# The place of the early row sums on VectorE in the last four expert pairs of an RWKV-7, convolution and mixture-of-experts step

## What is computed

```
h = silu(x @ w_gate[e]) * (x @ w_up[e]);  h = h * gate[token, e]
routed = sum over experts of h @ w_down[e]
y = residual + routed + shared;  out = rmsnorm(y)
```

## Time and profile before

| | |
|---|---|
| median of three runs | 1115.92 us (1115.02 to 1118.81) |
| the profiled execution | 1116.3 us |
| its span, first to last instruction | 1114.5 us |
| TensorE busy | 961.8 us, 86% of the span |
| VectorE busy | 536.9 us, 48% |
| GpSimd busy | 349.2 us, 31% |
| ScalarE busy | 226.5 us, 20% |
| mean granted TensorE clock | 0.94 of full speed |

### The profile page before, as it was taken

How to read it: one execution, slowest core, us unless ns; L and a number is a source line. 1 busy time by engine, 2 the same in 40 slices (tenths; PEclk the granted TensorE clock), 3 DMA queues, 4 the chain that set the end, 5 groups by cost and what they waited for, 6 DMA issues and landing times. The chain is left out here.

```text
span 1114.5 us, 17730 instructions
## 1 busy us (share of the span) xinstructions
PE 961.8 (86%) x7221; PEld 560.4 (50%) x7221; DVE 536.9 (48%) x1021; ACT 226.5 (20%) x469; POOL 349.2 (31%) x396
## 2 busy tenths in 40 slices
PE   5999999999999976598998888987988878789896
PEld 4878777877877774257433333333333323333231
DVE  2158759767875867945531101111112334434685
ACT  3241134125113412221111111111111111111012
POOL 0059609914960992001011101011012323312330
PEclk9999999999999999789999988989989888979999
DMA  8645244344524191654699999999999999999931
GB/s 224 187 127 182 96 131 167 110 131 137 181 96 134 61 345 35 246 234 162 262 367 416 418 417 412 412 406 402 403 398 408 400 392 364 403 415 402 390 99 40
DMA packets 98971, 295.65 MB, mean 265 GB/s; under 512 B 19602, under 2 KB 50900, under 8 KB 82231
## 3 DMA queue, kind: packets, MB, share of 16 engines
q1 hardware_dynamic: 80695, 254.02, 60.1%
q0 software_dynamic: 18192, 40.46, 9.7%
HBM read 284.12 MB, written 36.30 MB: 288 GB/s over the span
## 5 line engine op out<-in xcount | busy, mean ns | idle before, releaser
L1278 PE MATMUL bank<-big 64*64 64x64 f32 (+7 forms) x6778 | 905.7, 364 | 129.0 <-DMA big<-in_w_up 72.4
L1278 PEld LDWEIGHTS bank<-big 64*64 64x64 f32 (+3 forms) x6778 | 512.4, 150 | 473.9 <-issue 384.5
L1569 ACT ACTIVATE big<-bank 128x256 f32<-128x256 f32 (+6 forms) x284 | 121.7, 450 | 715.4 <-PE bank L1278 398.9
L1075 POOL DMA_INDIRECT big<-xg,big x32 | 32.4, 1012 | 405.5 <-PE bank L561 354.1
L919 DVE TENSOR_TENSOR big<-big,bank 128x256 f32<-128x256 f32 x32 | 13.5, 420 | 239.5 <-ACT big L1569 239.5
L2039 POOL TENSOR_SCALAR big<-big 128x256 f32<-128x256 f32 x120 | 126.8, 1057 | 1.7
L2051 POOL TENSOR_TENSOR big<-big 128x256 f32<-128x256 f32 x120 | 86.7, 723 | 0.3
L1835 DVE SCALAR_TENSOR_TENSOR big<-big 128x256 f32<-128x256 f32 x120 | 79.2, 660 | 4.1
L979 DVE SCALAR_TENSOR_TENSOR big<-big 128x1024 f32<-128x1024 f32 (+1 forms) x48 | 61.5, 1280 | 16.4 <-DMA big<-yrows,big 13.1
L1092 POOL DMA_INDIRECT big<-yrows,big x48 | 50.3, 1047 | 50.9 <-DVE big L979 28.5
L1569 ACT ACTIVATE big<-big 128x16 f32<-128x16 f32 (+6 forms) x95 | 42.5, 487 | 57.5 <-DVE big L1790 18.5
(11 more groups left out here) (163 smaller groups left out, 412.0 us busy)
## 6 DMA issues: line engine op xcount, KB each, us to landing
big<-in_w_gate SPq DMA_DIRECT2D x64, 1024.0 KB, 15.5
big<-in_w_up SPq DMA_DIRECT2D x64, 1024.0 KB, 20.4
big<-in_w_down SPq DMA_DIRECT2D x64, 1024.0 KB
big<-in_w_in SPq DMA_DIRECT2D x29, 1024.0 KB, 5.5
yrows<-big POOLq DMA_DIRECT2D x32, 512.0 KB, 3.7
big<-in_w_out SPq DMA_DIRECT2D x2, 2048.0 KB, 16.7
big<-in_state_wkv SPq DMA_DIRECT2D x32, 64.0 KB, 2.3
out_wkv_s<-big SPq DMA_DIRECT2D x32, 64.0 KB, 4.0
```

Source lines behind the costliest of these rows:

```text
L1075: pool.indirect_dma_start(out=x[0:n, :], out_offset=None, in_=xg, in_offset=bass.IndirectOffsetOnAxis(ap=idxu[0:n, col:col + 1], axis=0), ...
L1278: return nc.tensor.matmul(out_, lhsT=lhsT, rhs=rhs, start=start, stop=stop)
L1569: return nc.scalar.activation(out_, in_, f, **kw)
```

## The change

In pairs 28 to 31 the call of `add_early` is moved within VectorE's `pair(q)` from behind `add_late(q-2)` to behind `hidden(q)` and `take(q-1)`. The rows added in each pair, all waits, and the programs of the other engines stay as they are.

```diff
--- before.py
+++ after.py
@@ -936,12 +936,13 @@
                     late_gates(q + NLATE)
                 if q >= FIRST + 2:
                     add_late(q - 2)
-                    add_early(LATE_ROWS[q - FIRST - 2], LATE_ROWS[q - FIRST - 1])
                 if q == NPAIR - 1:
                     take(q - 1)
                 hidden(q)
                 if 0 < q < NPAIR - 1:
                     take(q - 1)
+                if q >= FIRST + 2:
+                    add_early(LATE_ROWS[q - FIRST - 2], LATE_ROWS[q - FIRST - 1])
                 if HALF + 3 <= q < HALF + 11:
                     add_early(TAKE_A * (q - HALF - 3), TAKE_A * (q - HALF - 2))
             def late_gates(q):
```

## The result

The changed kernel takes 1140.35 us in the median of four runs (1137.85 to 1144.32), the kernel before 1116.08 in the four beside it. The ratio is 1.022, with a 95% interval from 1.0189 to 1.025: slower by 24 us. The profiled execution took 1139.98 us, its span is 1138.2. The four last pairs carry it all, as the profiled executions show. From the start of `combine(26)`, TensorE's first work in pair 28, to the end of the span, it is 1114.5 - 1011.20 = 103.3 us before and 1138.2 - 1010.11 = 128.1 us after: 24.8 us more.

A forecast was written before the change was run, and what follows sets the result against it. TensorE was taken to set the end, VectorE mattering only where TensorE waits for it. Shifts of +4.74 us behind combine(28), +12.44 after pair 30 and +22.70 after pair 31 brought 1116.3 to 1139.0 us, range 1131 to 1147.

The forecast's parts named there:

- Pair 28's slip: In pair 28, three early sums delay the first late addition, so the combine's fourth product slips by 0.66 us.
- Pair 29's gain: combine(28) no longer waits for the copy: 3.77 us earlier less 0.66, plus 1.52 us at the lower clock saved.
- Row 32's gather: In pair 29, row 32's gather lands at 1056.35 after 6.3 us, so VectorE waits 1.66 us for it.
- The three waits: TensorE stands at the fourth product of combine(28), combine(29) and combine(30) for 7.85, 6.18 and 8.74 us.
- The clock: Half clock behind each long TensorE wait in combine(28), combine(29) and combine(30) costs 1.52 us.
- The estimate by the Trainium skill's rule: Half the throttled time behind each long TensorE wait is lost: 1.8 us each, giving 1139.9 us in all.
- Only the last pair pays: Late additions of pairs 29 and 30 are made up in time, only pair 31 costs: 1121.9 us, chance 0.07.
- The gathers are late in every pair: Late rows lengthen the sums by 6 us in pair 29 and some 3 in pair 30: 1148 us, chance 0.06.
- The faster rival: Pair 29's copy comes in time and the sums fit the gap before the fourth product: 1111.0 us, chance 0.03.
- No difference: Work moved one place in the ring costs the same, pair 29's 5.3 us gain balancing one wait: 1116, chance 0.02.

The follow-up runs named there:

- runs of single pairs: The change made in pair 29, 30 or 31 alone, against the kernel before: 1120.66 us (ratio 1.0025), 1124.58 us (one run), 1128.65 us (ratio 1.0106).
- the run with two and four sums: Kernel before, with two of pair 30's seven early sums moved behind the copy and four of pair 31's behind the inner product: 1123.1 us, one run.
- the run with filled waits: Changed kernel, TensorE forming 8, 6 and 9 unread products ahead of the fourth product of combine(28), combine(29), combine(30): 1135.39 us, ratio 1.0169 to kernel before.
- the last version: Kernel before, with the 24 early sums dealt out anew over pairs 28 to 31 and both places: 1110.26 us, ratio 0.9922.

## Why the prediction was right, point by point

It was: 1139.0 us for 1140.35 measured, by the mechanism on which it rested. One term of the sum was 1.8 us too small, and part of the closeness is chance. Its steps, against the profile:

- **Pair 28's slip.** 0.66 us predicted. The fourth product starts at 1032.26, 3.53 behind the `combine`'s start instead of 2.87: 0.66. The sum left out a small part: a cut group takes longer than an uncut one even at full clock, 2.92 + 6.53 = 9.45 us against 9.28, here and at each of the three long waits.
- **Pair 29's gain.** `combine(28)` was to start 3.11 us earlier, against pair 29's own start. From `combine(27)` to `combine(28)` it is 1048.13 - 1028.73 = 19.40 us now and was 22.39. The gain is 2.99, 0.12 less than forecast, which that part covers.
- **Row 32's gather.** A wait of 1.66 us at a landing of 6.3 us was predicted (its own terms, 1056.35 - 1047.89 - 6.85, give 1.61). Gathers 32 and 33 landed after 6.0 and 5.9 us, and their sums waited 1.61 us in all. Only 1.32 of it was row 32's; that row 33 would wait too was not forecast.
- **The three waits.** 7.85, 6.18 and 8.74 us predicted; 7.55, 6.01 and 8.78 measured, sum 22.3 for 22.8. The runs of single pairs gave 7.79, 6.10 and 8.78, so each is a matter of its own pair. The run with the sums in the middle of the late additions shows that TensorE needs the first three late additions, the banks, and not the sums themselves, and the run with two and four sums that there is a room and a price beyond it.
- **The clock.** This is the term that was mis-sized: 3 x 1.52 = 4.6 us predicted, 6.4 measured, by the run with filled waits. The value came from one wait of the kernel before, taken as the nearest. It was also the smallest price of its kind (below). The clock came to 1.8 us more than forecast, the cut groups to 0.5 and pair 29's gain to 0.1, the three waits to 0.4 less, so the tail grew by 24.8 us where 22.7 were forecast. The profiled execution, 1139.98 us, came out closer to 1139.0 than that because it reached the tail 1.1 us earlier, which is chance. By the medians the change cost 24.3 us.
- **The estimate by the Trainium skill's rule.** At 1.8 us a wait it stood nearer to the truth. The Trainium skill ("TensorE: Matmul & The Clock Gate", section "Terms") takes, at half rate, half the throttled time as the penalty. Counted from the first matmul behind the wait, it fits both traces: before, 1052.22 to about 1055.3, half of it 1.5 us for 1.52; after, 1058.60 to about 1063.3, half of it 2.3 us for 2.26. Counted from the clock's fall it does not, once a wait is long: after, the granted clock fell at about 1053.0, 2 us behind TensorE's last matmul at 1051.04, and half of the 10.3 us until 1063.3 would be 5.1. What the rows before could not tell is how long the low clock would last.
- **The rivals.** "Only the last pair pays" would have put 10.3 us at pair 31 and nothing at pairs 29 and 30; pair 30 alone costs 8.7. "The gathers are late in every pair" would have shown DMA waits before L980 in pair 30: there is none. The faster rival needed a sum of under 0.5 us, and L980 takes 1.27 to 1.30. "No difference" is excluded by the interval of the time.

## What to carry to other kernels

When work is moved on an engine with slack, look at who waits for the instruction that the work now stands ahead of, and count the room in time: the gap to that instruction and what the waiting engine has in hand (here three banks). Up to the room it costs nothing, beyond it each unit costs its own length, and if the waiting engine is TensorE, add the low clock behind each long wait, 1.5 to 3 us in these runs. A block that fits in no gap whole may fit when split: in pair 29, seven sums cost a wait in either place, 4.71 us in the old and 7.55 in the new, and in the last version one in the old place and two behind the copy did not. (Two more of that block were added in pair 28 and two in pair 30.)

## What the runs showed that I had not expected

What the low clock takes behind a wait of 4.6 us or more varied from 1.5 to 3.0 us, with no order by the wait's length. Behind waits of 4.71, 4.72, 4.76 and 5.21 us for the same copy, the same 28 matmuls took 10.80, 10.88, 12.27 and 11.66 us for 9.28. The first of these lines stands in the earlier trace rows and the last above; the other two are from TensorE's timelines of the run with pair 30 alone and of the run with two and four sums:

```profile
1051.88 10.88 PE L1281 MATMUL bank<-big 128*128 128x512 f32 x28 [4.72 <-DVE big L928]
...
1050.95 12.27 PE L1280 MATMUL bank<-big 128*128 128x512 f32 x28 [4.76 <-DVE big L928]
```

What differs is how long the clock stays at the lower level once TensorE works again: about 3.1 us in the kernel before, and about 6.1 in the last of these lines (0.50 until 1057, 0.95 in the microsecond from there). Why is open. Waits of 8.78 us cost 1.8 in one run and 2.7 in another. A price of the clock read from one wait should carry a range of about a microsecond to each side. Such differences, at this and at earlier waits, may go some way to the spread of 8 us between the kernel before's own runs (1114.55 to 1122.74 among 19), but how much of it they are was not measured.
